# One-core kernel of four layers with a routed expert stage: expert tables built for whole tables at once, and the norm passages reordered

## The reference, cut to what matters

```
# layers 0, 1                                        # layers 2, 3
h = rms_norm(x, g_pre) * (1 + sc) + sh               h = x * (1 + sc) + sh
y = mixer_or_ffn(h)                                  y = mixer_or_ffn(h)
x = x + gt * rms_norm(y, g_post)                     x = layer_norm(ALPHA * x + (1 + gt) * y, gain, bias)
```

```
logits = x @ w_router + b_router
top_vals, top_idx = lax.top_k(logits, 2)
combine = sum(one_hot(top_idx) * softmax(top_vals))
for e in range(8):
    out += combine[..., e] * ((silu(x @ w_gate[e]) * (x @ w_up[e])) @ w_down[e])
```

## Time and profile before

| what | value |
|---|---|
| time, three runs | 2508.34, 2511.90, 2511.92 us (median 2511.9) |
| profiled execution | 2508.86 us, of it the span 2507.0 us |
| PE, DVE, ACT, POOL busy | 2378.1, 1723.8, 1232.4, 647.0 us |
| mean granted TensorE clock | 0.975 of full speed |
| bytes read from HBM | 647.06 MB |

### The profile page before, as it was taken

How to read it: one execution, slowest core, us unless ns; L and a number is a source line. 1 busy time by engine, 2 the same in 40 slices (tenths; PEclk the granted TensorE clock), 3 DMA queues, 4 the chain that set the end, 5 groups by cost and what they waited for, 6 DMA issues and landing times. The chain is left out here.

```text
span 2507.0 us, 38211 instructions
## 1 busy us (share of the span) xinstructions
PE 2378.1 (95%) x15277; PEld 1962.7 (78%) x15277; DVE 1723.8 (69%) x2014; ACT 1232.4 (49%) x1317; POOL 647.0 (26%) x349
## 2 busy tenths in 40 slices
PE   6999999899999998999998799999999999999996
PEld 4875999785899775999876577888888888888774
DVE  2565677474876775675596587878787878786556
ACT  2334543443434223333213466776767677766552
POOL 0000000000950352940082123232323232323122
PEclk9999999999999999999999899999999999999998
DMA  9897765567785585685532398999999999998771
GB/s 337 269 350 236 260 210 167 157 197 251 242 260 173 177 273 172 222 265 177 168 111 85 137 330 287 364 352 364 351 365 351 363 352 359 357 359 320 261 274 71
DMA packets 416381, 650.06 MB, mean 259 GB/s; under 512 B 37018, under 2 KB 255222, under 8 KB 416246
## 3 DMA queue, kind: packets, MB, share of 16 engines
q1 hardware_dynamic: 389040, 633.12, 73.1%
q10 hardware_dynamic: 27206, 15.03, 2.2%
HBM read 647.06 MB, written 1.05 MB: 259 GB/s over the span
## 5 line engine op out<-in xcount | busy, mean ns | idle before, releaser
L1597 ACT ACTIVATE region_part<-ring 128x2048 fp32r<-128x2048 f32 x412 | 770.5, 1909 | 272.8 <-PE bank L873 188.6
L2594 DVE TENSOR_TENSOR ring_part<-ring,region_part 128x2048 fp32r<-128x2048 f32 x240 | 577.0, 2432 | 60.3 <-PE bank L1207 32.9
L873 PE MATMUL bank<-ring_part,region_part 128*128 128x512 f32 x1480 | 579.1, 391 | 0.0
L871 PE MATMUL bank<-region_part 128*128 128x512 f32 x1288 | 513.3, 399 | 13.2 <-DVE ring_part L2594 8.1
L872 PE MATMUL bank<-region_part 128*128 128x512 f32 x1152 | 449.9, 390 | 0.0
L1487 POOL TENSOR_TENSOR ring_part<-ring,region_part 128x2048 fp32r<-128x2048 f32 x48 | 247.2, 5158 | 521.6 <-ACT region_part L1597 435.0
L871 PE MATMUL bank<-xn_part,region_part 128*128 128x256 f32 x1152 | 328.0, 285 | 9.5 <-DVE hT_part L2226 8.2
L873 PE MATMUL bank<-hT_part,region_part 128*128 128x256 f32 x1152 | 326.3, 283 | 0.0
L872 PE MATMUL bank<-xn_part,ring_part 128*128 128x256 f32 x1152 | 326.2, 283 | 0.0
L873 PEld LDWEIGHTS bank<-ring_part,region_part 128*128 128x128 f32 x1480 | 278.5, 188 | 60.2
L871 PEld LDWEIGHTS bank<-region_part 128*128 128x128 f32 x1288 | 242.9, 189 | 73.0 <-issue 19.3
(11 more groups left out here) (383 smaller groups left out, 3909.5 us busy)
## 6 DMA issues: line engine op xcount, KB each, us to landing
ring<-in_moe_w_gate SPq DMA_DIRECT2D x112, 1024.0 KB, 5.1
ring<-in_moe_w_up SPq DMA_DIRECT2D x112, 1024.0 KB, 5.2
ring<-in_moe_w_down SPq DMA_DIRECT2D x112, 1024.0 KB, 4.9
ring<-in_w_ada SPq DMA_DIRECT2D x48, 1024.0 KB, 9.3
ring<-in_mod_w SPq DMA_DIRECT2D x48, 1024.0 KB, 6.8
ring<-in_w_in SPq DMA_DIRECT2D x44, 1024.0 KB, 5.7
ring<-in_w_up_act SPq DMA_DIRECT2D x22, 1024.0 KB, 5.5
ring<-in_w_up_lin SPq DMA_DIRECT2D x22, 1024.0 KB, 5.7
```

What stands on the lines that cost most here:

```text
L871: nc.tensor.matmul(o, split(a_hi), split(b_hi), start=start, stop=False, skip_group_check=True)
L873: return nc.tensor.matmul(o, split(a_hi), split(b_lo), start=False, stop=stop, skip_group_check=True)
L1597: return nc.scalar.activation(out_, in_, func, **kw).then_inc(*done(*event))
L2594: v.tensor_tensor(split(w), w, whole(hi), ALU.subtract).then_inc(*done("moe_lo", j, e))
```

## The change

1. **Expert tables.** The pairwise comparison in `route` is done once for both token tiles (128 columns for 64). `wide_expert` moves ahead of the first expert's chunk loop, behind `x_part("start")`. `wide_places` loses its second product and sum and stands at step 9 with `other_places`. The three `extra_turn` and `last_places` give way to `columns` (step 15) and `last_columns` (step 27), which work out the four last columns of the tables together; `turn_experts` goes from step 22 to 21 and raises `turns`.
2. **Passages of layers 0 and 1.** The gating of t = 1 is put between the steps of t = 0, and t = 0's scaled copy behind t = 1's variance.
3. **Passages of layers 2 and 3.** The gated y, the sum and the moments go by halves of 512 columns, the first half of t = 1 before `centred(0)`. PE does y of t = 1 by column halves in layer 2's and 3's mixers and in layer 2's feed-forward, and tells when the first is ready. POOL's `gains` wait for the last sum into x (`post`, 4) and no longer for `normed` of t = 1.

The diff, with the indentation cut and left-out lines marked:

```diff
 def out_second(l):
-    for t in range(NT):
+    for n in (2, 3):
+        out_tokens(l, n, 0)
+    if l < 2:
         for n in (2, 3):
-            out_tokens(l, n, t)
+            out_tokens(l, n, 1)
+        return
+    for c in range(2):
+        for n in (2, 3):
+            pe.wait_ge(*loaded(("out", l, n)))
+            for k in range(2):
+                m = nc.tensor.matmul(y_tiles[2 + c], hT[:, 2 * n + k, P:2 * P], chunk(("out", l, n))[:, k, c * 512:(c + 1) * 512],
+                                     start=False, stop=n + k == 4, skip_group_check=True)
+            if c:
+                m.then_inc(*done("pe_used", "out", l, n))
+        if c == 0:
+            m.then_inc(*done("pe_tile", "y", l, "mix"))
...
-    def down_part(f, t):
+    def down_part(f, t, cols=(0, 1)):
...
     def last_downs(gs):
-        for t in range(NT):
+        for t, cols in ((0, (0, 1)), (1, (0,)), (1, (1,))) if l == 2 else ((0, (0, 1)), (1, (0, 1))):
             for g in gs:
                 pe.wait_ge(*until("w_lo_down", l, g))
                 for f in (2 * g, 2 * g + 1):
-                    last = down_part(f, t)
-                if t:
+                    last = down_part(f, t, cols)
+                if t and cols[-1]:
                     last.then_inc(*done("pe_used", "down", l, 0, g))
                 elif g == gs[-1]:
-                    last.then_inc(*done("pe_used", "y", l, "ffn"))
+                    last.then_inc(*(done("pe_tile", "y", l, "ffn") if t else done("pe_used", "y", l, "ffn")))
...
     pool.wait_ge(*until(f"rows_{stage}{l}", 1))
-    pool.wait_ge(*until("normed", l, stage, 1))
+    pool.wait_ge(*until("post", l, stage, 4))
...
     gate = mod_gate[:, 0 if stage == "mix" else 1 + l % 2, :]
     nl, nstage = (l, "ffn") if stage == "mix" else (l + 1, "mix")
-    for t in range(NT):
...
+    def gated(t, c):
+        sl = slice(c * 512, (c + 1) * 512)
+        if c:
+            dve.wait_ge(*until(*y_ready(l, stage, t)))
+        else:
+            dve.wait_ge(*until("y_ssq", l, stage, 2 * t))
+        v.tensor_tensor(xn[:, t, sl], psum[bank_of["y", l, stage, 2 * t + c]], gate[:, sl], ALU.mult)\
+            .then_inc(*(done("y_gated", l, stage, t, 1) if c else link()))
+    def squared(t):
+        v.tensor_scalar(stat[:, 40 + t:41 + t], stat[:, 8 + 2 * t:9 + 2 * t], 1.0 / D, 1e-6, ALU.mult, ALU.add).then_inc(*link())
         dve.wait_ge(*until("y_ssq", l, stage, 2 * t + 1))
-        v.tensor_scalar(stat[:, 40 + t:41 + t], stat[:, 8 + 2 * t:9 + 2 * t], 1.0 / D, 1e-6, ALU.mult, ALU.add).then_inc(*link())
         after()
         v.scalar_tensor_tensor(stat[:, 42 + t:43 + t], stat[:, 9 + 2 * t:10 + 2 * t], 1.0 / D, stat[:, 40 + t:41 + t],
                                ALU.mult, ALU.add).then_inc(*done("variance", l, "post", stage, t))
+    def summed(t):
         dve.wait_ge(*until("rstd", l, "post", stage, t))
         v.scalar_tensor_tensor(x[:, t, :], xn[:, t, :], stat[:, 42 + t:43 + t], x[:, t, :], ALU.mult, ALU.add)\
             .then_inc(*done(*(("x_new", l, stage) if t else ("x_new_t", l, stage, 0))))
-        if nl < 2:
-            spread_of(nl, nstage, t)
-            if (nl, nstage, t) != (1, "mix", 1):
-                scaled(nl, nstage, t)
+    after()
+    gated(0, 1)
+    gated(0, 0)
+    squared(0)
+    summed(0)
+    gated(1, 1)
+    if nl < 2:
+        spread_of(nl, nstage, 0)
+    gated(1, 0)
+    squared(1)
+    if nl < 2:
+        scaled(nl, nstage, 0)
+    summed(1)
+    if nl < 2:
+        spread_of(nl, nstage, 1)
+        if (nl, nstage) != (1, "mix"):
+            scaled(nl, nstage, 1)
 def post_layer(l, stage):
     gate = mod_gate[:, 0 if stage == "mix" else 1 + l % 2, :]
     columns = ((56, 57, 58), (12, 13, 14))
-    def gated(t):
...
-    def moments(t):
+    def gated(t, c):
+        i, sl = 2 * t + c, slice(c * 512, (c + 1) * 512)
+        dve.wait_ge(*until(*(("pe_tile", "y", l, stage) if (t, c) == (1, 0) else y_ready(l, stage, t))))
+        v.scalar_tensor_tensor(xn[:, t, sl], gate[:, sl], 1.0, psum[bank_of["y", l, stage, i]], ALU.add, ALU.mult)\
+            .then_inc(*done("post", l, stage, i))
+        after_ = until("post", l, stage, i)
+        dve.wait_ge(*after_)
+        v.scalar_tensor_tensor(x[:, t, sl], x[:, t, sl], ALPHA, xn[:, t, sl], ALU.mult, ALU.add)\
+            .then_inc(*(done("post", l, stage, 4) if i == 3 else link()))
+        if i == 3:
+            dve.wait_ge(*until("post", l, stage, 4))
+        else:
+            after()
+        v.bn_stats(stat[:, 44 + 6 * c:50 + 6 * c], x[:, t, sl]).then_inc(*link())
+    def spread_in(t):
         mu, var, rs = columns[t]
...
         after()
         v.bn_aggr(stat[:, mu:mu + 2], stat[:, 44:56]).then_inc(*link())
         after()
...
     if (l, stage) != (2, "mix"):
         dve.wait_ge(*until("x_gained", *((l, "mix") if stage == "ffn" else (l - 1, "ffn")), 1))
-    for t in range(NT):
-        dve.wait_ge(*until(*y_ready(l, stage, t)))
-        gated(t)
-        moments(t)
-        centred(t)
+    gated(0, 0)
+    gated(0, 1)
+    spread_in(0)
+    gated(1, 0)
+    centred(0)
+    gated(1, 1)
+    spread_in(1)
+    centred(1)
...
         v.tensor_tensor(over, total, room, ALU.is_gt).then_inc(*link())
         after()
         v.tensor_tensor_scan(rank, one.broadcast_to([P, NE]), over, 0.0, ALU.mult, ALU.add).then_inc(*link())
-        v.tensor_scalar(room, wide, float(-OVER), None, ALU.mult).then_inc(*link())
+        v.tensor_scalar(room, wide, float(-OVER), float(-CAP), ALU.mult, ALU.add).then_inc(*link())
     def wide_places():
-        for i, what in enumerate((rank_of, cb)):
...
+        after()
+        v.tensor_tensor(mine, rank_of, wide.unsqueeze(1).broadcast_to([P, NT, NE]), ALU.mult).then_inc(*link())
+        after()
+        v.tensor_reduce(moe[:, 3, :, 0], mine, AX.X, ALU.add).then_inc(*link())
         v.tensor_scalar(over_iota.rearrange("p (r s) -> p r s", r=4), iota[:, 0:OVER].unsqueeze(1).broadcast_to([P, 4, OVER]),
                         float(CAP), None, ALU.add).then_inc(*link())
         after()
...
             after()
             v.tensor_tensor(to[:, :, 1:NE - 1], mine[:, :, 1:NE - 1], what[:, :, 1:NE - 1], ALU.add).then_inc(*link())
+    table = moe_pair.rearrange("p v a b -> p (v a b)")
+    extra = table[:, 0:32].rearrange("p (c e) -> p c e", c=EXTRA + 1)
+    column = table[:, 32:64].rearrange("p (c e) -> p c e", c=EXTRA + 1)
+    spare = table[:, 64:128]
+    def columns():
+        n = EXTRA + 1
+        each = lambda a: a.unsqueeze(1).broadcast_to([P, n, NE])
+        v.tensor_tensor(extra, each(rank), iota[:, 1:n + 1].unsqueeze(2).broadcast_to([P, n, NE]), ALU.is_equal).then_inc(*link())
+        v.tensor_scalar(ids[:, 0:n], iota[:, 0:n], rank[:, NE - 1:NE], None, ALU.is_equal).then_inc(*link())
+        after()
+        v.tensor_tensor(extra, extra, each(over), ALU.mult).then_inc(*link())
+        v.tensor_tensor(column, each(wide), ids[:, 0:n].unsqueeze(2).broadcast_to([P, n, NE]), ALU.mult).then_inc(*link())
+        after()
+        v.tensor_tensor(column, column, extra, ALU.add).then_inc(*link())
+        tmp = spare[:, 0:32].rearrange("p (c e) -> p c e", c=n)
+        v.tensor_tensor(tmp, extra, each(room), ALU.mult).then_inc(*link())
+        after()
+        v.tensor_reduce(stat[:, 48:48 + n], tmp, AX.X, ALU.add).then_inc(*link())
+        v.tensor_copy(extra[:, n - 1, :], wide).then_inc(*link())
+        after()
+    def last_columns():
+        n = EXTRA + 1
+        after()
+        wide_ = spare.rearrange("p (t c e) -> p t c e", t=NT, c=n)
+        for what, to in ((rank_of, place), (cb, weight)):
+            v.tensor_tensor(wide_, what.unsqueeze(2).broadcast_to([P, NT, n, NE]),
+                            column.unsqueeze(1).broadcast_to([P, NT, n, NE]), ALU.mult).then_inc(*link())
+            after()
+            v.tensor_reduce(to[:, :, NE - 1:TURNS], wide_, AX.X, ALU.add).then_inc(*link())
+            after()
+        v.tensor_tensor(place[:, :, NE - 1:TURNS], place[:, :, NE - 1:TURNS],
+                        stat[:, 48:48 + n].unsqueeze(1).broadcast_to([P, NT, n]), ALU.add).then_inc(*link())
     def turn_experts():
-        after()
+        n = EXTRA + 1
+        after()
+        tmp = spare[:, 0:32].rearrange("p (c e) -> p c e", c=n)
+        v.tensor_tensor(tmp, extra, iota[:, 0:NE].unsqueeze(1).broadcast_to([P, n, NE]), ALU.mult).then_inc(*link())
         v.tensor_scalar(ids, iota[:, 0:NE], -1.0, NE - 1.0, ALU.mult, ALU.add).then_inc(*link())
         after()
+        v.tensor_reduce(stat[:, 52:52 + n], tmp, AX.X, ALU.add).then_inc(*link())
         v.tensor_tensor(ids, ids, wide, ALU.mult).then_inc(*link())
-        v.tensor_tensor(hot[:, 1, :], wide, iota[:, 0:NE], ALU.mult).then_inc(*link())
         after()
         v.tensor_tensor(ids, ids, iota[:, 0:NE], ALU.add).then_inc(*link())
-        v.tensor_reduce(stat[:, 48:49], hot[:, 1, :], AX.X, ALU.add).then_inc(*link())
```

(79 more changed lines are left out.)

19 lines of the change are left out of this document (removed).

## The result

The changed kernel took 2493.4 us (median of four runs, 2492.8 to 2495.7) against 2511.9 for the one before: a ratio of 0.993, 95% interval 0.9917 to 0.9944, or 18.5 us less. The prediction was 2498, which is 13.9 less, with a range of 2491 to 2507. The profiled execution took 2492.95 us, 15.9 less than its counterpart, where the prediction's sum was 13.7 less. The difference is larger by the medians because the profiled execution before was 3.0 us under its median.

A forecast was written before the change was run, and what follows sets the result against it. PE was busy 95% of the span, with DVE the limit in the first expert. First expert -9.8, layers 0 and 1 -4.7, layers 2 and 3 +0.8 made -13.7 us: from 2511.9 to 2498.2, taken as 2498, range 2491 to 2507.

The forecast's parts named there:

- First expert, -9.8: First expert's chunk loop: two PE stalls of 3.68 us, smaller gaps and low clock go, less small costs: 9.8 us less.
- both starts: First expert: DVE's second `low_part` of two pairs now starts before POOL's subtraction, removing a 3.68 us stall each time.
- the gap near step 10: First expert: step 9 holds 4.0 us of DVE work for 3.2, leaving one PE gap of about 1 us.
- rival D: First expert: DVE wins one race and loses one, so one stall of 3.68 + 1.4 us stays: 2503 us; chance 0.15.
- Rival C: First expert: transfers hold it; if the DMA rate cannot rise, the 9.8 us stay: 2508 us; chance 0.06.
- The prediction's 375 GB/s: First expert without stalls: a chunk of 1.05 MB each 2.8 us would need this rate from HBM.
- Layers 0 and 1, -4.7: Passages of layers 0 and 1: 1.9 us less after each mixer, 0.9 after layer 0's feed-forward, nothing after layer 1's.
- at the higher one DVE and ACT get their first tiles about 0.4 sooner: After the mixers of layers 0 and 1: transposes at the 2.4 GHz clock, 1.09 us for 1.97, deliver first tiles earlier.
- Layer 2's mixer, -0.2: Passage after layer 2's mixer: the work by halves brings it 0.2 us sooner, with no block by POOL.
- The two copies let DVE start first: After layer 2's mixer: two copies let DVE start `centred(1)` before POOL's gains, so the 2.0 us hold is avoided.
- Layer 2's feed-forward, +2.8: Passage after layer 2's feed-forward: POOL's gains hold `centred(1)` 2.0 us, less 0.3 gained, plus 1.1 of lower clock.
- Layer 3, -1.8: After layer 3's mixer and in routing: +0.7 us at the transposes, -0.9 for the freed subtraction, -0.9 for the comparison.

The follow-up runs named there:

- the moved step: The kernel before with `other_places` moved from chunk step 18 to step 22 of the first expert, ahead of `turn_experts`: 2507.6 us.
- the delay of 1.6 us: The changed kernel with a chain of eight unused DVE additions of 8 columns at chunk step 18 of the first expert: 2497.0 us.
- delays of 0.8 us: The changed kernel with a chain of four unused DVE additions of 8 columns at chunk step 18 of the first expert: 2493.8 us.
- of memsets: The changed kernel with a chain of eight DVE memsets of 8 columns at chunk step 20 of the first expert: 2495.1 us.

## Why the prediction was right, and where its terms were off

- **First expert, -9.8, measured -9.2** (10.9 less the 1.7 of clock behind it). The expert itself gave 10.8 in all seven undisturbed traces with part 1; of that the clock took 1.2 to 1.6 back later in the span in seven of the ten traces with part 1, and nothing in the other three. Cause and place were right: both starts were won, by 1.2 us, and the gap near step 10 is 1.06 us for "about 1". That the stalls come from the order of two starts is shown from both sides, by the moved step and by the delay of 1.6 us. What the prediction didn't see is that losing is possible again at each of POOL's chunks, independently, as the moved step showed: rival D's chance of 0.15 had more behind it than one miss of 0.4.
- **Rival C** is out: 354 GB/s were moved, and PE waited for no transfer. The Trainium skill, "SBUF — State Buffer", section "A bandwidth-pool intuition that's wrong", gives about 358 GB/s for a core; this trace's first expert stays 1% below it, and 100 us of the loop behind it (1563 to 1663) went above it with 366. The prediction's 375 GB/s were not needed: in the window SP issued 37 chunks while PE used 42, and its issues waited for PE.
- **Layers 0 and 1, -4.7, read from the trace as -2.2, over all traces about -2, by medians -3.6 to -7.9.** The idle times came as forecast for the mixers (3.13 and 3.00 for 2.9). The step that failed is the clock: "at the higher one DVE and ACT get their first tiles about 0.4 sooner" came true after layer 1's mixer (1.09 us) and not after layer 0's (1.97). After layer 0's feed-forward t = 0's transposes wait 1.3 us longer, as costed, but the first products then ran partly at the lower clock (5.89 us for 5.35), which I had not counted. And after layer 1's feed-forward, where the prediction had "nothing", 0.7 us are lost: the second transposes there run at the lower clock (1.7 to 2.0 us for 1.09) in eight of nine traces with part 2 and in none of the five without, behind an idle of 2.04 us for 2.16.
- **Layer 2's mixer, -0.2, measured -1.6.** "The two copies let DVE start first" was true of `centred(1)` (0.81 us), and I stopped there. The earlier gains meet the next unit: its first wait grew by 2.15 us. Against it the gains were over sooner, so that two later waits of 1.17 and 0.57 went, and the clock was higher (0.69 for 0.61 over 22 us, 1.8 us). The sign of the sum came from terms that the prediction didn't have; -1.6 is at the large end of what the other traces with these gains show (-0.8 to -1.7).
- **Layer 2's feed-forward, +2.8, measured +1.7.** The block is 2.0 us, as in the earlier trace rows. "PE's idle grows from 3.66 to 5.4" failed: it is 2.33, because PE already waited 2.10 us for t = 0's tile (0.49 before) and transposed it at the lower clock (1.94 us). Most of the clock was lost there and not behind the second transposes (1.20 us), so little more than the block's 2.0 less the 0.3 gained was paid: 1.7.
- **Layer 3, -1.8, measured -1.8:** +0.8 at the transposes (0.7 forecast), and -2.6 in the routing (1.63 for the freed subtraction, 0.9 for the comparison; 1.6 and 0.9 forecast).
- **The rest, -3.1,** lies in unchanged code and is the clock of these two executions. The sum was within 2.5 us of the measured 16.2 partly by luck: layers 0 and 1 fell 2.5 short of their term and layer 2 came out 2.5 better than its two. Without the clock in unchanged code the change's own places add up to 13.1. By the medians the forecast was 4.6 us short (13.9 for 18.5), and no trace shows where that lies; the parts alone add up to 21.4.

## What to carry to other kernels

Where two engines exclude each other, list their starts at each meeting: a margin of tenths of a microsecond decides over a whole instruction of the other engine, and a few small instructions moved change it at every later meeting. Winning the start is not free either: the other engine then waits, and its user may too. When a wait is relaxed, follow the freed instruction past its first neighbour. Work whose result is not needed for a long time belongs where nothing waits for the other engine, which was worth more here than making it earlier or undoing that.

## What the runs showed of the hardware that was not expected

- A DVE addition of 8 columns, from SBUF to SBUF, stands behind a POOL subtraction like a large one (4.5 us); a memset of 8 columns and a product with one input in PSUM do not. The trace before had a first sign of it (1.93 us for 8 columns, 1.81 for 16). The Trainium skill, "SBUF — State Buffer", section "SBUF: two separate sides", has a lock for two-input and two-port instructions of DVE; these rows agree with it, and show that size is no excuse.
- POOL's memset of 0.95 us holds DVE's normalisation as its arithmetic does (1.41 for 0.81).
- The clock can fall without an idle of PE. Behind the changed kernel's first expert, with no wait of PE over 0.1 us for 45 us, PE did 32 products of 128 columns and 32 of 32 columns, and then ran at the lower clock for some 3.5 us (0.87 over 13.5). The same instructions ended at the lower clock in four of the fourteen traces (this one, the two with delays of 0.8 us and of memsets, the one with part 2 undone) and at 1.00 in the other ten.
- Unchanged code differs by 1.5 to 1.75 us from one execution to the next for the clock alone, as in the sixteen products of layer 2's mixer (5.24 us or 3.72). An effect of that size is read better from one stretch of many traces than from medians of the whole.
